# The opening of a two-block network by chunks of rows, its modulation sums spread anew, and its last four weight tiles by column halves, on one core

## The reference, cut to what matters

```python
def hybrid_layer(x, c, cos, sin, pre_g, post_g, w_ada, b_ada, w_in, w_out):   # two layers, x is 256 x 1024
    mod = jnp.einsum('bd,de->be', jax.nn.silu(c), w_ada) + b_ada
    shift, scale, gate = jnp.split(mod, 3, axis=-1)
    h = rms_norm(x, pre_g) * (1 + scale[:, None, :]) + shift[:, None, :]
    proj = jnp.einsum('bsd,de->bse', h, w_in)
    ...  # rotary embedding of q and k, two kinds of attention, silu gates
    y = rms_norm(jnp.einsum('bse,ed->bsd', jnp.concatenate([o_a, o_b], axis=-1), w_out), post_g)
    return x + gate[:, None, :] * y

def second_block(x, ...):                 # two more layers with their own modulation
    for l in range(DEPTH):
        x = macaron_half_ffn(x, ...)      # x + 0.5 * gate * swiglu(modulate(x))
        ...                               # mixer
        x = macaron_half_ffn(x, ...)
    return rms_norm_2(x, final_g)
```

## Time and profile before

| what | us |
|---|---|
| median of 3 runs | 1634.32 (1634.32 to 1634.64) |
| the profiled execution | 1635.31 |
| its span | 1633.5 |
| PE busy in it | 1607.6 (98%) |
| DVE busy | 1173.3 (72%) |
| ACT busy | 774.3 (47%) |
| POOL busy | 63.0 (4%) |

### The profile page before, as it was taken

One profiled execution on the slowest core, in us unless ns is written; L12 is line 12 of the kernel. 1 busy time (PEld: TensorE's weight loads), 2 busy tenths in 40 slices (PEclk: granted clock), 3 DMA queues, 4 the chain that ended last, 5 costly groups with the idle time before them and its releaser, 6 DMA issues.

```text
span 1633.5 us, 20618 instructions
## 1 busy us (share of the span) xinstructions
PE 1607.6 (98%) x7958; PEld 1325.4 (81%) x7958; DVE 1173.3 (72%) x1921; ACT 774.3 (47%) x1221; POOL 63.0 (4%) x95
## 2 busy tenths in 40 slices
PE   6999999999999999999999999999999999999998
PEld 5778777888888888887776888888888888888886
DVE  7778898748976666477645789867877758666654
ACT  4766565542221223254445555535554563554552
POOL 0000100010000000020001100001000100010000
PEclk9999999999999999999999999999999999999999
DMA  9866676325666665242122387866777585455551
GB/s 378 334 246 232 259 269 210 130 99 195 219 217 215 222 226 199 90 160 77 65 88 84 135 329 290 316 232 259 258 282 273 181 329 214 163 192 192 182 183 37
DMA packets 93187, 337.49 MB, mean 207 GB/s; under 512 B 10641, under 2 KB 11281, under 8 KB 92833
## 3 DMA queue, kind: packets, MB, share of 16 engines
q1 hardware_dynamic: 90848, 328.11, 56.1%
q0 software_dynamic: 2240, 8.06, 1.5%
HBM read 335.08 MB, written 1.05 MB: 206 GB/s over the span
## 4 chain that ended last, share of the span: by engine, by line
PE 54%; DVE 2%; issue 1%; ACT 0%; POOL 0%; DVEq 0%; POOLq 0%; ACTq 0%
PE bank L292 52%; PE bank L295 2%; DVE sb_tm L301 0%; DVE sb_XN L309 0%; ACT sb_arena L298 0%; ACT sb_XN L298 0%; DVE sb_X L301 0%; DVE sb_XN L301 0%; DVE sb_sg L316 0%; DVE sb_arena L319 0%; DVE sb_XC L301 0%; DVE sb_w8r L301 0%; DVE sb_w5r L301 0%; POOL sb_rstd L301 0%; DVE sb_arena L312 0%
## 5 line engine op out<-in xcount | busy, mean ns | idle before, releaser
L298 ACT ACTIVATE sb_hi<-sb_w 128x1024 fp32r<-128x1024 f32 x428 | 431.4, 1052 | 289.1 <-DMA sb_w<-in_w 242.3
L292 PE MATMUL bank<-sb_hT,sb_hi 128*128 128x512 f32 x1600 | 527.6, 394 | 0.0
L292 PE MATMUL bank<-sb_hi,sb_hT 128*128 128x512 f32 x1280 | 418.6, 398 | 3.8 <-ACT sb_hT L298 3.3
L292 PEld LDWEIGHTS bank<-sb_hT,sb_hi 128*128 128x128 f32 x1600 | 292.3, 188 | 58.4
L292 PEld LDWEIGHTS bank<-sb_hi,sb_hT 128*128 128x128 f32 x1280 | 241.2, 189 | 60.4 <-issue 7.7
L312 DVE CUSTOM_DVE_ANT_0 sb_w<-sb_w,sb_cb 128x1024 f32<-128x1024 f32 x144 | 174.7, 1218 | 0.0
L301 DVE TENSOR_TENSOR sb_sg<-bank,sb_sg 128x512 f32<-128x512 f32 (+1 forms) x90 | 58.9, 660 | 102.5 <-ACT sb_sg L298 80.7
L298 ACT ACTIVATE sb_sg<-bank 128x512 f32<-128x512 f32 (+1 forms) x98 | 54.9, 574 | 126.5 <-PE bank L292 122.7
L298 ACT ACTIVATE sb_arena<-bank 128x512 f32<-128x512 f32 (+1 forms) x108 | 58.2, 561 | 74.4 <-PE bank L295 38.8
L292 PE MATMUL bank<-sb_arena 128*128 128x64 f32 (+5 forms) x400 | 87.7, 345 | 0.5 <-DVE sb_arena L319 0.5
L301 DVE TENSOR_TENSOR sb_tm<-bank,sb_rows 128x512 f32<-128x512 f32 x40 | 27.6, 691 | 72.4 <-PE bank L292 69.6
(11 more groups left out here) (470 smaller groups left out, 3204.3 us busy)
## 6 DMA issues: line engine op xcount, KB each, us to landing
sb_w<-in_w SPq DMA_DIRECT2D x428, 512.0 KB, 4.2
sb_w<-in_mw SPq DMA_DIRECT2D x192, 512.0 KB, 4.6
sb_rows<-in_na_rpb POOLq DMA_DIRECT2D x16, 96.0 KB, 2.3
sb_X<-in_x SPq DMA_DIRECT2D x1, 1024.0 KB, 4.9
sb_cb<-in_cvec POOLq DMA_DIRECT2D x2, 512.0 KB, 6.9
sb_XC<-in_ctx POOLq DMA_DIRECT2D x1, 1024.0 KB, 9.7
sb_arena<-in_sg_ln_g POOLq DMA_DIRECT2D x1, 1024.0 KB, 6.2
sb_arena<-in_sg_ln_b POOLq DMA_DIRECT2D x1, 1024.0 KB, 9.5
```

Source lines behind the costliest of these rows:

```text
L292: return self.e.matmul(out, a, b, start=start, stop=stop)
L298: return self.e.activation(out, a, f, **kw)
```

## The change

Five things change together.

1. The order of loads: first one row of c (4 KB, `crow`) in place of its copy to 128 partitions, then x, and the two kinds of tiles alternate. TensorE spreads the row to all partitions by a product with ones (`pe_condition`), and ScalarE reads silu from the banks. The constant -1/2 is written by GpSimd (`minus_half`) and no longer loaded.
2. The opening of stage a0: ScalarE scales x (`act_first_rows`), GpSimd computes the angles (`pool_rope_tables`, where one fused step becomes two), chunk 0 goes its own way through VectorE (`dve_first_chunk`), chunk 1 through ScalarE (`act_first_chunk`), and TensorE does tiles 0 and 1 for chunk 0, then for chunk 1, then tiles 2 and 3 (`pe_first_tiles`). Tiles 4, 8 and 12 put their products with the low part of the activations last.
3. An activation of silu on a small tile stands first on ScalarE; the program then has one table load ahead of the opening instead of two.
4. `vector_times`: 30 row sums instead of 24 beside tiles 16 to 34, and 18 over tiles 43 to 70 instead of 24 over 40 to 66.
5. The end: the last four tiles for block 1 run by halves of 256 columns, the right half into another bank; the left half is added to x while the right one is multiplied, the squares of both halves are summed, and the last scaling is shared by VectorE and ScalarE.

```diff
-    for first, last, count in ((16, 34, 24), (40, 66, 24), (W_F00 + 8, W_MX - 10, 64), (W_F01 + 4, W_F10 - 10, 32),
+    for first, last, count in ((16, 34, 30), (43, 70, 18), (W_F00 + 8, W_MX - 10, 64), (W_F01 + 4, W_F10 - 10, 32),
...
-    for c in range(4):
-        out += [("m", 4 * c + i) for i in range(4)] + [("w", 4 * c + i) for i in range(4)]
+    out = [("m", 0), ("m", 1), ("w", 0), ("m", 2), ("m", 3), ("w", 1), ("w", 2), ("w", 3)]
+    out += [("m", n) for n in range(4, 8)]
+    for n in range(4, 16):
+        out += [("w", n)] + [("m", n + 4)] * (n < 12)
...
+            e.dma(crow[:, :], I["cvec"][0:1, :]).then_inc(LD["cb"].sem, LD["cb"].put(0, by=16))
             e.dma(X[:, :, :], I["x"].rearrange("(j p) d -> p j d", p=128)).then_inc(LD["x"].sem, LD["x"].put("x", by=16))
-            e.dma(CB[0][:, :], I["cvec"][0:1, :].partition_broadcast(128)).then_inc(LD["cb"].sem, LD["cb"].put(0, by=16))
-            e.dma(posi[:, :], I["positions"][:, :]).then_inc(LD["pos"].sem, LD["pos"].put(0, by=16))
...
+        def pe_first_tiles(e):
...
+            for u, k in ((0, 0), (1, 0), (0, 1), (1, 1), (2, 0), (2, 1), (3, 0), (3, 1)):
...
         def act_block1(e, l):
...
-                act_rope_tables(e)
+                act_first_rows(e)
+                act_tick(e, 0, 0)
...
+                act_tick(e, 0, 1)
+                act_first_chunk(e)
+                act_tick(e, 0, 3)
+                act_rope_tables(e)
...
         def pool_start(e):
+            e.memset(ones[:, :], 1.0).then_inc(PO.sem, PO.put("ones"))
+            e.memset(minus_half[:, :], -0.5).then_inc(PO.sem, PO.put("minus_half"))
             pool_rstd(e, "a0")
-            e.wait_ge(*done(USED, 5))
+            pool_rope_tables(e)
+            e.wait_ge(*done(USED, 9))
...
+        def pe_last_tiles(e, t0, key, parts, banks):
...
+            for half in range(2):
+                c = slice(half * 256, half * 256 + 256)
+                o = (bank[0] if half else banks[1]).ap[:, c]
+                for k in range(7, 11):
...
+                    for x in range(2):
+                        kc = 2 * k + x
+                        e.mm(o, ah(kc, 1), h[:, x, c], half == 1 and kc == 14, False)
+                        e.mm(o, ah(kc, 1), l[:, x, c], False, False)
+                        m = e.mm(o, al(kc, 1), h[:, x, c], False, kc == 21)
```

More of the change, by code:

```diff
@@ L687, in pe_norm @@
                     for i, j in enumerate(js):
[L688 removed]
+                        e.wait_ge(*done(AE if s == "a0" else DE, "xn", s, c2 // 2, j))
                         c = (h * len(js) + i) * 128
@@ L776, in h_ready @@
             p, c2 = 0 if s in JOINT else j, kc // 2
+            if s == "a0" and kc == 0:
+                return done(DE, "chunk", part)
             if s == "a0":
@@ L958, in pe_block1 @@
                 key, at, first, last = b1_banks(l, u)
+                if l == 0 and u < 4:
+                    continue
                 if first:
-                    BANK[key] = [(TB if l == 0 and u in (2, 3) else AB).take() for _ in range(2)]
+                    BANK[key] = [AB.take() for _ in range(2)]
                 if l == 1 and u < 4:
@@ L968, in pe_block1 @@
                         parts, ready = [cols_of(t) for t in yT[g]], split_ready("y", l, g)
-                    pe_unit(e, t0 + u, key, parts, at, BANK[key], (0, 1), ready, first, last)
+                    pieces = ("hl", "a") if l == 0 and u in (4, 8, 12) else ("hla",)
+                    for terms in pieces:
+                        pe_unit(e, t0 + u, key, parts, at, BANK[key], (0, 1), ready, first, last and "a" in terms,
+                                used="a" in terms, terms=terms)
                 if last:
@@ new lines, in dve_end @@
+            residual(0)
+            dve_mean(e, "fin", 0, [done(SQ, "fin", 0, nh) for nh in range(2)])
+            key, g, sums_ = ("d", "m12", 0, 1), G[GROW["m12"]], ssq[:, NS["fin"], 1, :]
+            e.wait_ge(*done(ACC, *key, "left"))
+            e.wait_ge(RES, RES.n)
+            e.tt(TM[1][:, :], BANK[key][1].ap[:, :], g[:, 512:1024], ALU.mult).then_inc(DE.sem, DE.put("last", 0))
+            e.wait_ge(DE, DE.n)
+            e.tt(X[:, 1, 512:1024], X[:, 1, 512:1024], TM[1][:, :], ALU.add).then_inc(RES.sem, RES.put("m12", 0, 1, "half", 0))
@@ new lines, in dve_end @@
+            e.wait_ge(*done(PO, "rstd", "fin", 0))
+            e.stt(XN[:, 0, 512:1024], X[:, 0, 512:1024], rstd[:, NS["fin"], 0:1], PG[:, 512:1024], ALU.mult,
+                  ALU.mult).then_inc(DE.sem, DE.put("final", 0, 1))
+            e.wait_ge(*done(SQ, "fin", 1, 1, "left"))
+            e.tt(sums_[:, 0:1], sums_[:, 0:1], hs[:, 0:1], ALU.add).then_inc(DE.sem, DE.put("last", "sum"))
+            e.wait_ge(*ended(*key, 1))
+            e.wait_ge(DE, DE.n)
+            e.wait_ge(RES, RES.n)
@@ new lines, in dve_end @@
+            e.tt(TM[1][:, 256:512], bank[0].ap[:, 256:512], g[:, 768:1024], ALU.mult).then_inc(DE.sem, DE.put("last", 1))
+            e.wait_ge(DE, DE.n)
+            e.tt(X[:, 1, 768:1024], X[:, 1, 768:1024], TM[1][:, 256:512], ALU.add).then_inc(
+                RES.sem, RES.put("m12", 0, 1, "half", 1))
+            dve_mean(e, "fin", 1, [done(SQ, "fin", 1, nh) for nh in range(2)])
+            e.wait_ge(*done(PO, "rstd", "fin", 1))
+            e.stt(XN[:, 1, 512:1024], X[:, 1, 512:1024], rstd[:, NS["fin"], 1:2], PG[:, 512:1024], ALU.mult,
+                  ALU.mult).then_inc(DE.sem, DE.put("final", 1, 1))
```

195 lines of the change are left out of this document (152 added, 43 removed).

## The result

| | median, us | lowest to highest | runs |
|---|---|---|---|
| before | 1634.49 | 1634.22 to 1635.65 | 20 |
| changed | 1631.74 | 1630.86 to 1634.97 | 20 |

The ratio is 0.9984, with a 95% interval of 0.9977 to 0.9990. The change makes the kernel 2.75 us faster; I had forecast 5.6, and the median lies 0.06 us inside the upper end of my range, on the slow side of the forecast itself (1627.5 to 1630.0). About half of the expected gain is missing. The changed kernel also scatters more: 4.1 us between its fastest and its slowest run (2.3 without one run at 1634.97), where the kernel before has 1.4.

A forecast was written before the change was run, and what follows sets the result against it. TensorE's dense stream bounds the kernel, so time is its start, fixed content and a tail. Opening -4.65 and end -0.9 sum to -5.55: 1634.32 becomes 1628.8, stated as 1628.7, range 1626.6 to 1631.8.

The forecast's parts named there:

- The start of the stream and tile 4: Opening of a0: first product at 13.3 instead of 18.99, tile 4 at 28.1 instead of 32.76, a gain of 4.65.
- the gap ahead of tile 4: Opening: TensorE, done with tiles 0 to 3 at 26.7, waits 1.4 us for VectorE's list before tile 4.
- The angles: Opening: 14 small GpSimd steps from 8.5 on, ending at 21 to 23, covered ahead of tile 4.
- C: Opening: GpSimd's angle steps wait for VectorE passes and block ScalarE, losing the opening's gain; 1634.3, chance 0.10.
- The reference point: Tile 4's start before, 32.76 in the profiled execution, which lay 0.99 above the median.
- Rival B: Opening: TensorE's products keep the 0.41 distance longer, costing tile 4 1.1 or 2.6; 1630.2 to 1631.6, chance 0.13.
- The row sums: Six more beside tiles 16 to 34 fit VectorE's idle time: counted at nothing, bounds +7.3 and -0.7.
- Rival D: Tiles 16 to 34: six row sums delay the heads' small steps, TensorE stops 7.3 us; 1636.0, chance 0.05.
- The sign that I had given for it: A new gap on TensorE between 60 and 145 us would show row sums delaying the heads.
- The end: Block 1's last tiles by halves, squares and scaling shared: 0.9 us less from last products to output.
- the two passes: End: two VectorE passes after the last product go from 512 to 256 columns, -0.5.
- the scaling and issues: End: sharing the two scalings gives -0.5, of which 0.2 comes back through SP's two issues, net -0.3.

The follow-up runs named there:

- experiment 5: Changed kernel with the angles of the rotary tables back on VectorE, behind the low part of tile 0: 1633.97 us.
- experiment 3: Kernel before with only the new row-sum places (30 beside tiles 16 to 34, 18 over 43 to 70): 1636.47 us, ratio 1.0012.
- experiment 1: Changed kernel with the row sums' places as before (24 beside tiles 16 to 34, 24 over 40 to 66): 1630.00 us.
- experiment 2: Changed kernel with its 18 later row sums over tiles 43 to 66 instead of 43 to 70: 1630.11 us.
- experiment 4: Changed kernel with the end as before (last four tiles whole for block 1, both scalings on VectorE): 1632.24 us.
- experiment 9: Changed kernel with the row sums' places and the end as before, so only the new opening: 1630.26 us.

## Why the prediction came out as it did

*The start of the stream and tile 4: right.* First product 13.08 for 13.3, tile 4 27.68 for 28.1, VectorE's list as the cause (experiment 5). That the gap ahead of tile 4 came out as well, 1.32 for 1.4, is in part luck: only three products at the long distance in place of 14 spared TensorE 1.8 us, and waits for two weight tiles that I had not seen (0.63 and 0.23 idle, with slower restarts 1.4) took most of it again. The angles ended at 20.8, so C did not happen. There is luck in this number too: I had 21 to 23 from a start at 8.5, but the positions landed only at 10.9, and the steps took 9.9 us where I had 12.5 to 14.5. By the rule of the exclusive lock in the Trainium skill, "SBUF — State Buffer", "SBUF: two separate sides", each step that meets a pass waits for its whole rest. The trace agrees, 1.18 where 0.29 is the price alone. Six of the 14 steps took 1.0 us or more; the others met none, or only its last part.

*The reference point: slightly wrong.* I took 32.76 as tile 4's start before and subtracted the difference from the median. That execution had a late rise of TensorE's distance (experiment 3). Against the median the opening is worth 4.3, not 4.65. Two errors partly cancel in this term: tile 4 came 0.4 earlier than I had it, and the reference was some 0.8 late. The row that warned me was in my own text: the profiled execution lay 0.99 above the median, and I took this off the total without asking which term was late. Rival B was aimed at this, but in the wrong kernel: with the changed opening the products keep the long distance only until 14.5 in the changed kernel's profile, and only until 13.3 in experiments 1 and 2, where I had counted 14 of them; and the difference makes nothing there, since tile 4 waits for `sb_hT` in all three. B's sum was off as well: its losses of 1.1 and 2.6 on 1628.7 give 1629.8 to 1631.3, not 1630.2 to 1631.6.

*The row sums: the step that failed.* I wrote "counted at nothing" from VectorE's idle share beside tiles 16 to 34, and looked at the six that were added there. What cost most was the other half of the same edit, the range of the second group from 40-66 to 43-70: a place, not an amount. The measured price is 1.7 (1631.74 - 1630.00) to 2.1 (experiment 3). Rival D had the mechanism, a row sum ahead of a step on a head's small tile, with the wrong stage, too high a price (7.3) and 5% of the chance. The sign that I had given for it, a new gap between 60 and 145 us, could not show it: the new waits stand at 150.7 and 287.9. Of the six added sums the price is the lost lead of the loads: 0.8 to 1.3 us in five traces with 30 sums, nothing in the sixth, and in the medians of experiments 1 and 2 only 0.1.

*The end: right in kind, half in size.* Term by term, from the rows above and the earlier trace rows: the products +0.31 for my +0.15 (first product to the first step behind the last, 5.95 and 5.64; a product of 256 columns takes 0.12 there and not 0.117); the two passes -0.53 for -0.5; the square -0.22 for -0.25; the scaling and issues 0.0 for -0.3: the scaling ends 0.66 sooner, the two issues in a row give 0.44 back and the landing 0.22. The sum is -0.44. The trace of experiment 4 has 0.46, and the medians of experiments 9 and 1 differ by 0.3.

*The sum.* -4.3 - 0.4 + 1.7 to 2.1 = -2.6 to -3.0, measured -2.75. Without the row sums the forecast of 1628.7 would have met 1630.0, still 1.3 off, of which the opening and the end explain 0.85.

## What to carry to other kernels

A stretch with idle time on an engine does not make added work there free: look at what stands behind each added pass in the engine's queue, and move the last one off the place where another engine waits for a short step. When a table of places changes, check its ends before its counts, and count a tile that serves two targets as two passes. Before a difference is taken against one profiled execution, ask which of its terms made that execution differ from the median.

## What the runs showed of the hardware

- The moment at which TensorE's products go over from 0.43 to 0.23 us differs between executions of the same opening: 22.7 and 25.0 with the first product at 18.97 and 18.99, 3.3 us after the transposes; 13.3 to 15.4 with the first product at 12.95 to 13.17, right behind the transposes. The window of before around its late rise shows a granted clock of 1.00 all the same.
- Fourteen small GpSimd steps beside a dense VectorE took 0.70 us each, where those that met no pass took 0.19 to 0.29, and VectorE's pitch stayed at 1.14 to 1.16.
- Two output pieces issued on two queues at the same time ended no earlier than in a row 0.5 us apart: 2.8 and 2.3 us from the last issue to the end.
